# Value weights first in both mixers, in fp32, one token block at a time

## The reference

```python
h = rmsnorm(x, attn_norm_w)
proj = h @ w_in        # q,k,v for the delta rule | z | b, a | q, k, v of the differential attention
qkv_la = silu(causal_conv(qkv_la, conv_w))              # 4 taps
o_la = gated_delta_rule(q_la, k_la, v_la, g, beta)      # chunked, triangular solve
lam = exp(sum(lq1*lk1)) - exp(sum(lq2*lk2)) + lam_init
o_d = diff_attention(q_d, k_d, v_d, lam, rel_bias)      # softmax 1 - lam * softmax 2
x = x + concat(norm(o_la)*silu(z), norm(o_d)) @ w_out
x = x + (silu(gate) * up) @ w_down                      # hidden width 2816, then a final norm
```

## Time and profile before

| | |
|---|---|
| three runs | 862.53, 857.8, 858.37 us; median 858.37 |
| profiled execution | 859.9 us, span of the instructions 858.1 us |
| mean granted TensorE clock | 0.953 |
| PE busy | 774.1 us (90%) |
| DVE busy | 585.2 us (68%) |
| ACT busy | 389.9 us (45%) |
| POOL busy | 133.0 us (16%) |
| weights | 268 transfers of 512 KB |

### The profile page before, as it was taken

How to read it: one execution, slowest core, us unless ns; L and a number is a source line. 1 busy time by engine, 2 the same in 40 slices (tenths; PEclk the granted TensorE clock), 3 DMA queues, 4 the chain that set the end, 5 groups by cost and what they waited for, 6 DMA issues and landing times.

```text
span 858.1 us, 13056 instructions
## 1 busy us (share of the span) xinstructions
PE 774.1 (90%) x5140; PEld 703.9 (82%) x5140; DVE 585.2 (68%) x935; ACT 389.9 (45%) x652; POOL 133.0 (16%) x76
## 2 busy tenths in 40 slices
PE   3969999798979999999978989999974999999995
PEld 2967898796779999999948978788964999999994
DVE  4675887555547868788757887556866576676664
ACT  5444223463435353534543434428353646555552
POOL 1202000002012222212232000000120121122220
PEclk9978999899879999999979999999996999999998
DMA  7662543233376888888823531344452355645531
GB/s 267 216 224 102 171 127 120 74 99 99 99 306 223 273 289 270 282 287 305 307 69 119 176 125 53 122 140 172 154 179 91 123 199 170 205 167 192 179 117 50
DMA packets 40382, 148.93 MB, mean 174 GB/s; under 512 B 4480, under 2 KB 4480, under 8 KB 39936
## 3 DMA queue, kind: packets, MB, share of 16 engines
q1 hardware_dynamic: 39456, 142.62, 49.3%
q10 hardware_dynamic: 864, 5.47, 1.6%
HBM read 147.02 MB, written 1.05 MB: 173 GB/s over the span
## 4 chain that ended last, share of the span: by engine, by line
PE 68%; DVE 11%; issue 10%; ACT 6%; POOL 3%; DMA 1%; POOLq 0%; DVEq 0%; ACTq 0%
PE bank L818 12%; PE bank L821 12%; PE bank L819 12%; PE bank L835 6%; PE bank L845 5%; PE bank L843 5%; PE bank L846 5%; PE bank L973 4%; ACT whi L1701 2%; DVE wlo L1196 2%; ACT XN L1701 2%; DVE arena L1202 2%; DVE XN L1202 2%; DVE arena L1196 2%; POOL small L1996 1%
## 5 line engine op out<-in xcount | busy, mean ns | idle before, releaser
L818 PE MATMUL bank<-hh,whi 128*128 128x256 f32 x1024 | 298.6, 292 | 12.1 <-ACT hh L1701 6.6
L819 PE MATMUL bank<-hl,whi 128*128 128x256 f32 x1024 | 295.1, 288 | 0.0
L821 PE MATMUL bank<-hh,wlo 128*128 128x256 f32 x1024 | 295.0, 288 | 0.0
L1196 DVE TENSOR_TENSOR wlo<-raw,whi 128x1024 fp32r<-128x1024 f32 x164 | 225.1, 1393 | 63.3 <-ACT whi L1701 63.0
L1701 ACT ACTIVATE whi<-raw 128x1024 fp32r<-128x1024 f32 x204 | 204.7, 1047 | 38.5 <-PE bank L821 17.4
L818 PEld LDWEIGHTS bank<-hh,whi 128*128 128x128 f32 x1024 | 202.0, 197 | 18.1 <-issue 15.1
L819 PEld LDWEIGHTS bank<-hl,whi 128*128 128x128 f32 x1024 | 202.2, 197 | 1.5
L821 PEld LDWEIGHTS bank<-hh,wlo 128*128 128x128 f32 x1024 | 201.9, 197 | 0.0
L1996 POOL TENSOR_TENSOR wlo<-raw,whi 128x1024 fp32r<-128x1024 f32 x40 | 105.4, 2636 | 474.8 <-ACT whi L1701 474.8
L1701 ACT ACTIVATE arena<-bank 128x256 f32<-128x256 f32 (+2 forms) x65 | 26.7, 420 | 115.3 <-PE bank L821 79.2
L1202 DVE SCALAR_TENSOR_TENSOR arena<-bank,cols,arena 128x255 f32<-128x255 f32 (+3 forms) x138 | 58.9, 479 | 26.7 <-ACT arena L1701 25.1
(11 more groups left out here) (163 smaller groups left out, 943.0 us busy)
## 6 DMA issues: line engine op xcount, KB each, us to landing
raw<-w_dram SPq DMA_DIRECT2D x268, 512.0 KB, 4.4
arena<-rows_dram ACTq DMA_DIRECT2D x1, 1792.0 KB, 6.4
X<-x_dram SPq DMA_DIRECT2D x2, 512.0 KB, 6.3
arena<-rows_dram ACTq DMA_DIRECT2D x1, 1024.0 KB, 10.2
arena<-bias_dram ACTq DMA_DIRECT2D x1, 1024.0 KB, 13.0
out_dram<-X SPq DMA_DIRECT2D x4, 256.0 KB, 2.0
const<-const_dram ACTq DMA_DIRECT2D x1, 704.0 KB, 5.8
arena<-bias_dram ACTq DMA_DIRECT2D x1, 512.0 KB, 6.5
```

What stands on the lines that cost most here:

```text
L818: e.matmul(o, a, hh[:, k, :], start=(k == 0), stop=False)
L819: e.matmul(o, a, hl[:, k, :], start=False, stop=False)
L821: ins = e.matmul(o, wlo[:, s, k * 128:k * 128 + 128], hh[:, k, :], start=False, stop=(k == 7))
L1196: return e.tensor_tensor(out, a, b, op)
```

## The change

- The four value units stand at the head of each mixer's part of the stream and have a kind of their own, "w", which is not split. `values` multiplies raw weights with `h32` in fp32, one 512-column matmul per k and token block, first all four units for block 0, then all four for block 1. A unit's slot is given up after block 1.
- In the first mixer, block 0's first unit goes ahead of the second block's transposes. `h32` is now also written for the first norm. `vd` follows the convolutions, and the flags `vd` and `v2` are gone.
- In the second mixer, block 0's values stand ahead of `mod`, and block 1's after `turn(5)` and `gate_rows`; these two have changed places.
- The identity is fetched alone, and the ten masks later, in `split_ba`, with a semaphore of their own.
- Lambda's product is made in `split_ba`; its matmul stands at the head of `attention1`.
- `P.share` is empty in the first mixer from the start.

```diff
@@ stream()
+    units += [("w", "w_in_v", u) for u in range(4)]
     units += [("s", "w_in", f) for f in range(8)]
     units += [("s", "w_in_qk", f) for f in (0, 4)]
-    units += [("v", "w_in_v", u) for u in range(4)]
@@
+    units += [("w", "w_in_2v", u) for u in range(4)]
     units += [("s", "w_in_2", 12 + n + 4 * m) for n in range(4) for m in range(2)]
-    units += [("s", "w_in_2", 4 * m) for m in range(2)]
-    units += [("v", "w_in_2v", u) for u in range(4)]
-    units += [("s", "w_in_2", n + 4 * m) for n in range(1, 4) for m in range(2)]
+    units += [("s", "w_in_2", n + 4 * m) for n in range(4) for m in range(2)]
@@ plan(): moving_v
+        ids = [P.unit("w", name, u, lead=0) for u in range(4)]
+        for b in range(2):
+            for u, i in enumerate(ids):
+                P.of[i] = (tag, u, norm)
+                P.step("values", i, b)
+                if b and u < 3:
+                    P.uses(i)
+                elif b:
+                    P.fills_bank(i, tag + "1")
+                if u == 0 or (u == 3 and b == 0):
                     yield
@@ plan(): first mixer
-    P.side = [4, 5, 6, 7, 2, 3]
+    P.share = ()
...
-    P.need(0, lead=0)
     turn(0)
-    first_four(0, ("cv0", "cv2"), "w_in", (0, 1, 2, 3))
+    values = moving_v("v1", "w_in_v", 0)
+    next(values)
+    turn(1)
+    next(values)
+    P.need(P.mm[P.order[P.next - 1] + 1], lead=2)
+    finish(values)
     P.step("split_ba")
-    P.step("conv", 0)
-    P.step("conv", 2)
-    for f in (4, 6):
+    for f in (0, 2, 4, 6):
         finish(pair(f"cv{f}", "w_in", (f, f + 1), ("h", 0)))
         P.step("conv", f)
     bank = P.take(hold=True)
+    P.step("vd")
     P.fill("ba", bank)
     P.step("ba")
-    P.fill("lam")
-    P.step("lam")
@@ attention1
+        P.fill("lam")
+        P.step("lam")
+        yield
@@ second mixer
+    values = moving_v("v2", "w_in_2v", 2)
+    next(values)
+    next(values)
     P.fill("mod34")
     P.step("mod", 1)
+    turn(5)
     for n in range(4):
         P.fill(f"gt{n}")
     P.step("gate_rows")
-    first_four(2, ("glu0", "glu1"), "w_in_2", (12, 16, 13, 17))
+    P.need(P.mm[P.order[P.next - 1] + 1], lead=1)
+    finish(values)
+    P.step("v2")
@@ tensor engine
+            def values(i, b):
...
+                for n in range(2):
+                    k = 2 * u + n
+                    wait_after(f"turn{2 * norm + b}{k // 4}")
+                    ins = e.matmul(banks[2 + b][:, :], h32[:, k, tok(b)], raw[:, i % RAW, 512 * n:512 * n + 512],
+                                   start=(k == 0), stop=(k == 7))
@@ scalar engine
-                e.dma_start(const[:, :, :], const_d[:, :, :]).then_inc(sems["const"], 16)
+                e.dma_start(const[:, 0, :], const_d[:, 0, :]).then_inc(sems["const"], 16)
...
             def split_ba():
+                e.dma_start(const[:, 1:, :], const_d[:, 1:, :]).then_inc(sems["masks"], 16)
```

More of the change, by code:

```diff
@@ L119, in __init__ @@
         self.order = {i: n for n, i in enumerate(self.mm)}
-        self.split = [i for i in self.mm if self.units[i][0] != "n"]
+        self.split = [i for i in self.mm if self.units[i][0] not in "nw"]
         self.place = {i: n for n, i in enumerate(self.split)}
@@ L166, in prepare @@
                 self.ada[i] = len(self.ada) + 1
-            elif self.units[i][0] != "n":
+            elif i in self.place:
                 sem = "lo_pool" if self.place[i] % 4 in self.share else "lo_dve"
@@ L268, in moving_v @@
         P.fill(tag + "1", 3)
-        for u in range(4):
-            i = P.unit("v", name, u)
-            P.of[i] = (tag, u, norm)
-            for n in range(2):
-                P.step("movv", i, n)
-                if n == 0:
-                    yield
-            if u < 3:
-                P.uses(i)
-            else:
-                P.fills_bank(i, tag + "1")
-            yield
+        ids = [P.unit("w", name, u, lead=0) for u in range(4)]
[8 more added lines that the diff above has]
+                if u == 0 or (u == 3 and b == 0):
+                    yield
     def rows(q, m):
@@ L314, in main1 @@
         yield from qk(0)
-        yield from moving_v("v1", "w_in_v", 0)
-        P.step("vd")
-        flags.add("vd")
         yield from qk(1)
@@ L421, in attention1 @@
             yield
-            while "vd" not in flags:
-                yield
             if n < 8:
@@ L442, in attention1 @@
             P.step("head", b)
-    P.share = ()
     turns(main1(), delta(), attention1(), (0, 1, 2, 0, 2, 1, 0, 1, 2, 0))
@@ L483, in plan @@
     P.step("gate_rows")
-    first_four(2, ("glu0", "glu1"), "w_in_2", (12, 16, 13, 17))
+    P.need(P.mm[P.order[P.next - 1] + 1], lead=1)
+    finish(values)
+    P.step("v2")
+    P.step("biases2")
+    for n in (0, 1):
+        finish(pair(f"glu{n}", "w_in_2", (12 + n, 16 + n), ("h", 2)))
     P.side = [4, 5, 6, 7]
-    P.step("biases2")
     def main2():
@@ L494, in main2 @@
         for n in range(4):
-            if n == 1:
-                yield from moving_v("v2", "w_in_2v", 2)
-                P.step("v2")
-                flags.add("v2")
             yield from pair(f"qq{n}", "w_in_2", (n, n + 4), ("h", 2))
@@ L527, in attention2 @@
             if n < 8:
-                while ("qk2", n // 2) not in flags or "v2" not in flags:
+                while ("qk2", n // 2) not in flags:
                     yield
@@ L602 @@
 PAIRS = [(0, 0), (1, 1), (0, 1)]
-SEMS = """x0 x1 const cols bias1 rows gtb bias2 out00 out01 out10 out11 hi lo_dve lo_pool used ada
+SEMS = """x0 x1 const masks cols bias1 rows gtb bias2 out00 out01 out10 out11 hi lo_dve lo_pool used ada
 pconst sq ssum rpow xnd xna h_hi h_lo xw sc gt wb wbl csilu cva cvd qkv b1m lam gate gate_act dsq rnorm em atri
@@ L846, in rows_by @@
                 return e.matmul(o, ll[:, k, t0], whi[:, s, c:c + 512], start=False, stop=last)
-            def movv(i, n):
+            def values(i, b):
                 tag, u, norm = P.of[i]
-                k = 2 * u + n
-                if k == 0:
-                    open_bank(tag + "0")
-                    open_bank(tag + "1")
-                w.wait_ge("h_hi", 4 * norm + 4)
-                w.wait_ge("h_lo", 4 * norm + 4)
-                for b in range(2):
-                    ins = rows_by(i, banks[2 + b][:, :], hh, hl, k, tok(b), 512 * n, k == 0, k == 7)
-                    if k == 7:
-                        filled(ins, f"{tag}{b}")
-                if n == 1 and u < 3:
+                if u == 0:
+                    open_bank(f"{tag}{b}")
+                w.wait_ge(*fetched(i))
+                for n in range(2):
[3 more added lines that the diff above has]
+                                   start=(k == 0), stop=(k == 7))
+                if u == 3:
+                    filled(ins, f"{tag}{b}")
+                elif b:
                     done(i, ins)
@@ L1168, in _ @@
             does = {
-                "start": start, "turn": turn, "stat": stat, "whole": whole, "movv": movv, "mov": mov, "four": four, "ba": ba,
+                "start": start, "turn": turn, "stat": stat, "whole": whole, "values": values, "mov": mov, "four": four, "ba": ba,
                 "turn_ba": turn_ba, "lam": lam_, "norms": norms, "decay": decay, "kk": kk, "kq": kq, "lev_first": lev_first,
```

21 lines of the change are left out of this document (12 added, 9 removed).

## The result

| | median, us | ratio to before | profiled span, us |
|---|---|---|---|
| before | 859.43 | 1 | 858.1 |
| after | 882.02 (879.7 to 884.51) | 1.026 [1.022, 1.030] | 882.7 |

Slower by 2.6%, 24 us above the forecast of 857.6 and outside its range. The profiled execution is the longest of four; in later profiles with the same start the norms' matmul stood at 76.6 to 78.4, here at 79.2, so about 2 us of what follows is scatter of the start.

What follows compares the result with a forecast made beforehand. It took PE as the bound, with DVE in stretches of the first mixer. Terms +6.6 - 10.6 - 3.8 - 4 + 11 = -0.8 us on an execution of 859.9, 1.5 above the runs' median, gave 857.6; range 847.5 to 866.5.

Steps and rivals of the forecast that it cites:

- Value matmuls in the gap: Start of the first mixer: first value matmul at 11.3 us, values ending at 28.3, 0.85 us per matmul at full clock.
- Start, +6.6: First mixer up to the norms: norms' matmul at 72.5 instead of 65.91, +6.6 us, bounds +3 and +9.
- 2 to 3 us of waits for ACT's high copies: Term of the first mixer's start: DVE's waits between about 32.8 us and the copy for beta at 62.2.
- Lambda's matmul: First mixer, at 54.69 us: PE's 7.04 us wait for lambda's product is gone; beta's copy and the gates are late next.
- Norms to modulation, -10.6: First mixer, norms to the modulation's matmul: -11.1 for work gone, -1.5, +1, +2.5 and -1.5, sum -10.6 us.
- I had +1: First mixer behind the norms: attention's first heads fall where DVE has no slack, +1 us.
- A gap has a second price: General premise: after about 4 us idle PE runs at its lower level; at 0.50, 4 us do 2 us of work.
- Rival (2): First mixer becomes DVE-bound: start +9, full stretch +4 instead of +1, sum +4.6, 863.0 us; chance 0.24.
- Boundary, -3.8: Start of the second mixer: first block's values fill PE's gaps, first plain pair at 462.4, -3.8 us, bounds -5.5 and -1.
- Attention's first wait, -4: Second mixer: 3.5 us of PE's 4.09 us wait and 1.7 of slow clock go, -4 us, bounds -5 and 0.
- Tail, +11: End of the second mixer: main work ends before the 31-tap convolution, 10.3 us idle added, +11 us, bounds +6.5 and +14.4.

Runs made afterwards that it cites:

- e11: After, with the first mixer's values behind the beta projection, unit by unit, gates' steps among them, masks at the start, GpSimd's share as before: 874.4 us.
- e2: After's first mixer with before's second mixer: 874.8 us, ratio to before 1.017.
- e1: Before with one edit, lambda's matmul moved into attention's turn: 860.0 us, ratio to before 0.998.
- o5: Before without 36 of the 48 value matmuls of the first mixer: 858.8 us against 860.0 for before, measured beside it.
- e8: After, with 56 thrown-away matmuls filling PE's wait ahead of the norms: 882.6 us, ratio to before 1.028.
- e4: After with another pattern of turns in the second mixer, seven convolution turns for four of main work instead of five: 870.6 us.
- o2: Second mixer of after with e4's pattern; first mixer mostly in before's order, fp32 values in the turns ahead of the first pair, lambda moved: 892.0 us.
- e5: After, with the masks issued at the start, right behind the columns: 880.9 us, ratio to before 1.026.
- e7: After, with the modulation's weight units five places later in the stream: 877.0 us, ratio to before 1.020.
- o6: After, with 44 thrown-away matmuls ahead of the norms and 24 ahead of the last attention values: 880.9 us, ratio to before 1.024.
- e3: Before's first mixer with after's second mixer: 869.6 us, ratio to before 1.010.
- e9: After with the edits of e6 and e7 together: 876.8 us, ratio to before 1.018.
- o1: After with another first-mixer pattern, main work, delta rule and attention four turns each in twelve: 887.5 us, ratio to before 1.031.
- e6: After, with both token blocks of a first-mixer value unit taken before the next unit: 880.1 us, ratio to before 1.024.

## Why the prediction was wrong, point by point

**Value matmuls in the gap: right.** First at 11.20 (forecast 11.3), and the first weight matmul behind them at 28.4 (28.3). In e11, at a clock of 1.00, twelve of them (24 records) took 10.57 us:

```profile
49.58 10.57 PE L874 MATMUL bank<-raw,arena 128*128 128x512 f32 x24
```

That is 0.88 each, where I had 0.85. The Trainium skill (FP8 and Floating Point Precision, TensorE Precision Notes), with its four passes, came to an estimate of 0.91 from the fp32r row; the measurement lies between the two, and the difference from 0.85 is about half a microsecond per mixer.

**Start, +6.6 (bounds +3, +9): mis-sized.** It measured +13.3, and +11 in e2. The mechanism was the one named (held slots, more modulation steps, no GpSimd), but the term "2 to 3 us of waits for ACT's high copies" failed. From 32.8 to the copy for beta at 68.67 DVE was busy for 28.0 us, where I had 27.2, and idle for 7.9. That is nearly the whole error: from the copy to the gates' first step took 6.9 us (I had 6.8), and from there to the norms 3.7 (3.5). I had the fetches start at 23.2 and did not ask when they land: the high copies that wait for them come 5 to 8 us apart (27.24, 35.30, 40.16), with modulation units between them in the ring. No drain showed at the table load, as I had read from the earlier trace rows: the load at 28.46 takes 1.28 and the next activation starts at 29.75.

**Lambda's matmul: gone, and worth nothing.** I counted the 7.04 us nowhere as a gain of its own, which e1 bears out.

**Norms to modulation, -10.6: the step that failed.** It measured +4.5. I subtracted 11.1 us of PE work from a stretch because PE was mostly busy in it. The work did go (13.2 us by the two windows). But most of the value matmuls stood in the 22.5 us between the norms and the level step, and o5 shows the kernel to be at most 2.2 us shorter without 8 us of them. That is the step: work that covered a wait was counted as time. Two things then made this piece 29.0 us long. The clock: norms 6.99 us where the earlier trace rows has 5.37, D matrices 3.75 where before took 2.10; e8, which ran both at full clock, is 5 us shorter here. And DVE: kk to level step took 10.0 us (98.17 to 108.22), before 7.4 (81.02 to 88.39). DVE's timeline has about 1.2 us of the attention's softmax there, for which I had +1, and a wait of 1.42 for a high copy. It is not the clock: at full clock, e8 took 10.6. The rule about the clock was in my own text ("A gap has a second price"), and I applied it to the tail; ahead of the norms I forecast no wait of PE, and so priced none. Rival (2), which "decides once the gates' first step comes later than about 71 us", was the true branch (75.6), but it added 3 us to this stretch where 15 were due.

**Boundary, -3.8: right in kind, somewhat small.** From the first transpose (451.51) to the first plain pair (478.84) 27.3 us; before 32.5 with the same work (433.70 to 455.08, and 11.1). That is -5.2, inside its bounds.

**Attention's first wait, -4: not kept.** The wait fell from 4.09 to 1.57, less far than forecast (3.5 of it was to go). But up to the last gate pair nothing is left of it (-0.1). The high copy behind the value units waits 7.40 us for its weights at 477.89, and waits of 0.93 and 1.09 stand around the attention's first heads. This trade is argued from the rows; no run takes it apart.

**Tail, +11: right.** +11.2 up to the third attention output unit, idle added 9.9 us (11.25 - 1.33) where I had 10.3. e4 took it back with one pattern. This is the mechanism as forecast, not only its number.

**The sum.** My forecast was in the middle of terms of both signs, and one, -10.6, rested on a bound that I had not tested. With +4.5 in its place, the start at +11 and attention's wait at nothing, the same sum gives 859.9 + 11 + 4.5 - 5.2 + 11.2 = 881.4. The start at +11 is e2's; with the 13.3 of the profiled execution it is 883.7 for 884.5. What remains open: why moving the values behind the beta projection (e11) lengthens the stretch from the norms to the modulation by some 6 to 9 us, and why more turns for the delta rule lengthen it further. The rows show idle and slow time in place of work each time; which engine's chain sets it between 88 and 215 us was not isolated.

## What to carry to other kernels

A busy engine is not yet the bound of a stretch. Before work is subtracted from a stretch, ask what the stretch would last without it: a run that leaves the work out (o5) answers for one kernel what a sum of durations could not. Idle time and time at the lower clock belong in one column, since the second hides the first in the busy share. When work leaves a hand-made interleaving, the pattern was fitted to it: e4 changed one tuple for 11.4 us, but the same idea in the first mixer cost 5, so such a pattern is measured, not reasoned. And in this code a unit that waits unsplit in the ring holds a slot until its last use; the price seems to be paid by whoever is next in the queue that fetches (12.96 us in o2).

## What was unexpected of the hardware

The clock is not the same in executions of the same instructions. From the mean to the end, after, e5, e7, e8 and o6 took 280.2 to 280.4 us at a clock of 0.94; e3, e9 and o1, with the same instructions there, took 282.8 to 282.9 at 0.93, and e6 282.8 at 0.92. So a gain of 4 us at the norms (e6) can reach the end as 2. And in after PE ran at a clock of 0.51 for the 17 us behind a wait of 6.75, though it was busy for 93% of them; in e9, behind a wait of 6.74, the norms ran as slowly but the D matrices at full clock again.
